# Gate and up products of four feed-forwards as seven block products, inner channels in four chunks

## What is computed

```python
D_FF_2 = 2816
def rmsnorm(x, g):
    xf = x.astype(jnp.float32)
    y = xf * lax.rsqrt(jnp.mean(xf * xf, axis=-1, keepdims=True) + EPS_2)
    return (y * g.astype(jnp.float32)).astype(x.dtype)
def swiglu_2(x, w_gate, w_up, w_down):
    return (jax.nn.silu(x @ w_gate) * (x @ w_up)) @ w_down
...
        h = h + 0.5 * swiglu_2(rmsnorm(h, ffn1_norm[i]), ffn1_w_gate[i], ffn1_w_up[i], ffn1_w_down[i])
...
        h = h + 0.5 * swiglu_2(rmsnorm(h, ffn2_norm[i]), ffn2_w_gate[i], ffn2_w_up[i], ffn2_w_down[i])
```

## Time and profile before

| | |
|---|---|
| median of three runs | 3580.78 us |
| the profiled execution's own time | 3585.51 us |
| its span, first to last instruction | 3583.7 us |
| instructions in the trace | 41702 |
| granted TensorE clock, mean | 0.992 of full |
| read from HBM | 288.22 MB, 81 GB/s over the span |

### The profile page before, as it was taken

One profiled execution on the slowest core, in us unless ns is written; L12 is line 12 of the kernel. 1 busy time (PEld: TensorE's weight loads), 2 busy tenths in 40 slices (PEclk: granted clock), 3 DMA queues, 4 the chain that ended last, 5 costly groups with the idle time before them and its releaser, 6 DMA issues. The chain is left out here.

```text
span 3583.7 us, 41702 instructions
## 1 busy us (share of the span) xinstructions
PE 3504.6 (98%) x15716; PEld 2778.8 (78%) x15740; DVE 1573.3 (44%) x2139; ACT 1285.5 (36%) x1802; POOL 443.9 (12%) x366
## 2 busy tenths in 40 slices
PE   9999999999999999999999999999999999999998
PEld 7787788877778886888876688887888886688886
DVE  3386433356643334333366733325333256733335
ACT  4243422234532224332343533225332333533324
POOL 0000111000211100221000022102221000022102
PEclk9999999999999999999999999999999999999999
DMA  4201233222022331333220233313333220133322
GB/s 146 88 1 30 82 94 103 103 71 77 30 82 94 101 104 59 96 97 110 81 72 18 65 96 97 116 57 97 97 96 107 82 84 18 53 95 99 111 71 77
DMA packets 78029, 292.06 MB, mean 81 GB/s; under 512 B 8656, under 2 KB 11472, under 8 KB 77648
## 3 DMA queue, kind: packets, MB, share of 16 engines
q1 hardware_dynamic: 77328, 289.31, 25.3%
q10 hardware_dynamic: 576, 1.05, 0.1%
HBM read 288.22 MB, written 2.10 MB: 81 GB/s over the span
## 5 line engine op out<-in xcount | busy, mean ns | idle before, releaser
L157 DVE TENSOR_TENSOR w_low<-w_raw,w_high 128x1024 fp32r<-128x1024 f32 (+4 forms) x513 | 672.5, 1311 | 1524.3 <-ACT w_high L152 1524.2
L191 PE MATMUL bank<-x_high,w_high 128*128 128x512 f32 x2856 | 1119.1, 392 | 18.8 <-DVE w_low L157 9.2
L193 PE MATMUL bank<-x_high,w_low 128*128 128x512 f32 x2856 | 1112.2, 389 | 0.0
L192 PE MATMUL bank<-x_low,w_high 128*128 128x512 f32 x2856 | 1111.9, 389 | 0.0
L152 ACT CAST w_high<-w_raw 128x1024 fp32r<-128x1024 f32 (+4 forms) x513 | 555.0, 1082 | 846.9 <-PE bank L193 838.9
L191 PEld LDWEIGHTS bank<-x_high,w_high 128*128 128x128 f32 x2856 | 536.5, 188 | 144.1 <-DVE w_low L157 14.0
L193 PEld LDWEIGHTS bank<-x_high,w_low 128*128 128x128 f32 x2856 | 536.3, 188 | 111.9
L192 PEld LDWEIGHTS bank<-x_low,w_high 128*128 128x128 f32 x2856 | 536.5, 188 | 111.3 <-issue 1.7
L191 PE MATMUL bank<-hidden_high,w_high 128*128 128x512 f32 x1056 | 410.8, 389 | 0.0
L192 PE MATMUL bank<-hidden_low,w_high 128*128 128x512 f32 x1056 | 410.8, 389 | 0.0
L193 PE MATMUL bank<-hidden_high,w_low 128*128 128x512 f32 x1056 | 410.8, 389 | 0.0
(11 more groups left out here) (543 smaller groups left out, 3473.5 us busy)
## 6 DMA issues: line engine op xcount, KB each, us to landing
w_raw<-in_stream SPq DMA_DIRECT2D x381, 512.0 KB, 3.5
w_raw<-in_stream SPq DMA_DIRECT2D x96, 704.0 KB, 4.0
w_raw<-in_stream SPq DMA_DIRECT2D x16, 384.0 KB, 3.1
w_raw<-in_stream SPq DMA_DIRECT2D x4, 576.0 KB, 3.7
dft_positions<-in_dft SPq DMA_DIRECT2D x2, 1024.0 KB, 4.7
w_raw<-in_stream SPq DMA_DIRECT2D x16, 128.0 KB, 2.0
out<-result SPq DMA_DIRECT2D x4, 512.0 KB, 2.7
h<-in_x ACTq DMA_DIRECT2D x4, 256.0 KB, 6.3
```

Of the source, the lines that this page charges most:

```text
L157: self.nc.vector.tensor_tensor(self.lo[:, j % 2, 0:size], self.raw[:, j % RAW_SLOTS, 0:size], self.hi[:, j % 2, 0:size].bitcast(F32), ALU. ...
L191: nc.tensor.matmul(out, lhs[0], rhs[0], start=start, stop=False)
L192: nc.tensor.matmul(out, lhs[0], rhs[1], start=False, stop=False)
L193: return nc.tensor.matmul(out, lhs[1], rhs[0], start=False, stop=stop)
```

## The change

In the four stages the first two pairs of tiles (`CLASSIC`) stay as they were. The other twenty are computed as a product of 2 by 2 blocks with seven block products and not eight: block rows are the gate tile and the up tile, inner blocks the two halves of the input channels, block columns the two halves of the tokens. A pair's four weight blocks of 128 x 512 are `a11`, `a12` (gate) and `a21`, `a22` (up). VectorE makes four sums of them (`sum_one` to `sum_four`, three of them in the raw slots), seven of these eight blocks (a unit each) are split by ScalarE and VectorE into rings of six, and a block product is 4 x 3 matmuls of 256 columns. The four matching sums of the input are made once per stage from a fresh normalised copy of `h` (`x_made`). Partial results are taken from PSUM by ScalarE (`copy_out`, four of 256 columns) and put together by VectorE (`gate_left`, `up_right`, `gate_right`). The hidden tile's product is two operations of 256 columns.

The 22 pairs are cut into chunks of 6, 6, 5 and 5; behind each chunk come its 8 down jobs (768 or 640 columns), each 18 or 15 matmuls into `bank[6]` or `bank[7]`, and each is added to `h`. The stage is written out without hardware loops. The weight stream is packed in the new order. Before each chunk behind the first, the splits and sums of the next chunk's first pair are made beside the last down jobs. What each GpSimd instruction does stays: two of 512 columns per pair.

```diff
+CHUNKS = (6, 6, 5, 5)
+CLASSIC = 2
+UNITS = 6
...
-def rms_ffn_stage(nc, C, scale, gain=None, summed=None, after=None, p_dram=None):
+def rms_ffn_stage(nc, C, scale, norm, gain=None, summed=None, after=None, p_dram=None):
...
+        hid = sb("hidden_parts", [P, max(CHUNKS), 2, T], F32R)
+        hhi, hlo = hid[:, :, 0, :], hid[:, :, 1, :]
+        thi, tlo = (sb(n, [P, 4, HALF_T, HALF], F32R) for n in ("x_sums_high", "x_sums_low"))
+        uhi, ulo = (sb(n, [P, UNITS, HALF_T * P], F32R) for n in ("units_high", "units_low"))
+        s_one = sb("w_sum", [P, HALF_T * P])
+        part = sb("products", [P, 4, HALF])
+        p1, u2, p5, u3 = (part[:, i, :] for i in range(4))
...
+        t_raw = [x_upper[:, :, left], x_upper[:, :, right], x_lower[:, :, right], x_lower[:, :, left]]
+        T1, T3, T2, T4 = range(4)
...
+        def unit_raw(f, kind):
+            a11, a12, a21, a22 = blocks(f)
+            return (a11, a12, a11, s_one[:, :], a21, a12, a22)[kind]
...
+                def product(f, kind, bank, high, low, start):
+                    u = unit_at(f, kind)
+                    pe.wait_ge(S.unit_low, 7 * strassen(f) + kind + 1)
+                    for q in range(HALF_T):
+                        whi, wlo = (w[:, u, q * P:(q + 1) * P] for w in (uhi, ulo))
+                        first, last = start and q == 0, q == HALF_T - 1
+                        nc.tensor.matmul(bank, whi, high[:, q, :], start=first, stop=False, skip_group_check=True)
+                        nc.tensor.matmul(bank, whi, low[:, q, :], start=False, stop=False, skip_group_check=True)
+                        mm = nc.tensor.matmul(bank, wlo, high[:, q, :], start=False, stop=last, skip_group_check=True)
+                    mm.then_inc(S.used, 1)
+                def pair(f):
+                    g = strassen(f)
+                    a, b, e = (C.bank[3 * (f % 2) + i][:, left] for i in range(3))
+                    upper, lower = slice(0, HALF_T), slice(HALF_T, DT)
+                    pe.wait_ge(S.hid_ready, f - 1)
+                    product(f, 0, a, C.xhi[:, upper, left], C.xlo[:, upper, left], True)
+                    if g == 0:
+                        pe.wait_ge(S.gate_in, 2)
+                    product(f, 1, e, C.xhi[:, lower, left], C.xlo[:, lower, left], True)
+                    pe.wait_ge(S.copied, 4 * g + 1)
+                    if g == 0:
+                        pe.wait_ge(S.t_low, T2 + 1)
+                    product(f, 2, a, thi[:, T2, :, :], tlo[:, T2, :, :], False)
+                    product(f, 3, b, thi[:, T1, :, :], tlo[:, T1, :, :], True)
+                    pe.wait_ge(S.copied, 4 * g + 2)
+                    product(f, 4, a, thi[:, T3, :, :], tlo[:, T3, :, :], False)
+                    pe.wait_ge(S.copied, 4 * g + 3)
+                    product(f, 5, b, C.xhi[:, lower, right], C.xlo[:, lower, right], False)
+                    pe.wait_ge(S.copied, 4 * g + 4)
+                    if g == 0:
+                        pe.wait_ge(S.t_low, T4 + 1)
+                    product(f, 6, a, thi[:, T4, :, :], tlo[:, T4, :, :], False)
...
+                for f in range(CLASSIC):
+                    classic(f, 0)
+                    classic(f, 1)
+                for c, n in enumerate(CHUNKS):
+                    for f in range(max(CLASSIC, first_pair(c)), first_pair(c + 1)):
+                        pair(f)
+                    down(c, 0, range(0, n - 1))
+                    down(c, 1, range(0, 3))
+                    down(c, 0, range(n - 1, n))
+                    down(c, 1, range(3, n))
+                    for d in range(2, DT):
+                        down(c, d, range(n))
                 keep_warm(nc, C, C.bank[0], 10)
...
+                def unit(f, kind):
+                    g = strassen(f)
+                    u = 7 * g + kind
+                    if kind in (0, 1):
+                        arrived(act, up_job(f, 0))
+                    elif kind == 6:
+                        arrived(act, up_job(f, 1))
+                    else:
+                        act.wait_ge(S.summed, 4 * g + (3, 1, 2, 4)[kind - 2])
+                    if u >= UNITS:
+                        act.wait_ge(S.used, u - UNITS + 1)
+                    nc.scalar.copy(uhi[:, u % UNITS, :], unit_raw(f, kind)).then_inc(S.unit_high, 1)
...
+                for t in range(DT):
+                    at = x_upper if t < HALF_T else x_lower
+                    nc.scalar.activation(at[:, t % HALF_T, :], C.h[:, t, :], ACT.Identity,
+                                         scale=norm(t)).then_inc(S.x_made, 1)
+                high(2, 2)
+                rstd_chain(nc, C, act, S, C.bank[summed or 6])
+                silu(0)
+                sums_high(T1)
+                sums_high(T3)
+                high(3, 3)
+                sums_high(T2)
+                sums_high(T4)
+                hidden_high(0)
+                f = CLASSIC
+                unit(f, 0)
+                unit(f, 1)
+                silu(1)
+                for kind in range(2, UNITS):
+                    unit(f, kind)
+                hidden_high(1)
+                for c, n in enumerate(CHUNKS):
+                    for f in range(max(CLASSIC, first_pair(c)), first_pair(c + 1)):
+                        last = f == first_pair(c + 1) - 1
+                        i, j = 2 * CLASSIC + DT * c, down_job(c, 0)
+                        bank = [C.bank[3 * (f % 2) + i] for i in range(3)]
+                        if f > CLASSIC:
+                            act.wait_ge(S.added, 3 * strassen(f))
+                        copy_out(f, 1, bank[0], p1)
+                        if f > first_pair(c) and f > CLASSIC:
+                            silu(f - 1)
+                        unit(f, 6)
+                        if last:
+                            high(i, j)
+                        else:
+                            act.wait_ge(S.used, 7 * strassen(f) + 2)
+                            unit(f + 1, 0)
+                        copy_out(f, 3, bank[0], u2)
+                        if not last:
+                            unit(f + 1, 1)
+                        copy_out(f, 4, bank[1], p5)
+                        if last:
+                            high(i + 1, j + 1)
+                        else:
+                            unit(f + 1, 2)
+                        if f > CLASSIC:
+                            act.wait_ge(S.hid_ready, f)
+                        copy_out(f, 5, bank[0], u3)
+                        if not last:
+                            unit(f + 1, 3)
+                        if f > first_pair(c) and f > CLASSIC:
+                            hidden_high(f - 1)
+                        if not last:
+                            unit(f + 1, 4)
+                            unit(f + 1, 5)
+                    silu(f)
+                    hidden_high(f)
+                    for d in range(DT):
+                        if d + 2 < DT:
+                            high(2 * CLASSIC + DT * c + d + 2, down_job(c, d + 2))
+                        elif c == len(CHUNKS) - 1 and d == DT - 2 and base + jobs < len(W.sizes):
+                            high(2 * CLASSIC + DT * (c + 1), jobs)
+                        if c < len(CHUNKS) - 1 and d == DT - 3:
+                            for kind in range(UNITS):
+                                unit(first_pair(c + 1), kind)
+                        if c == len(CHUNKS) - 1:
+                            act.wait_ge(S.residual_done, DT * c + d + 1)
+                            after.high(nc, C, act, S, d)
+                            after.square(nc, C, act, S, d, gated)
...
+                for f in range(FT):
+                    pool.wait_ge(S.gate_ready, f + 1)
+                    nc.gpsimd.tensor_tensor(gated[:, f % 2, :], gated[:, f % 2, :], C.rstd[:, :],
                                             ALU.mult).then_inc(S.gate_scaled, 1)
-                    pool.wait_ge(S.hid_high, u + 1 + 4 * k)
-                    at = bass.ds(u + 4 * k, 1)
-                    nc.gpsimd.tensor_tensor(hlo[:, at, :], hidden[:, u % 2:u % 2 + 1, :],
-                                            hhi[:, at, :].bitcast(F32), ALU.subtract).then_inc(S.hid_low, 1)
-                repeat(pool, FT, finish)
...
...
+                def sum_one(f):
+                    nc.vector.tensor_tensor(s_one[:, :], a21, a22, ALU.add).then_inc(S.summed, 1)
+                def sum_three(f):
+                    nc.vector.tensor_tensor(a21, a11, a21, ALU.subtract).then_inc(S.summed, 1)
+                def sum_two(f):
+                    nc.vector.tensor_tensor(a11, s_one[:, :], a11, ALU.subtract).then_inc(S.summed, 1)
+                def sum_four(f):
+                    nc.vector.tensor_tensor(a12, a12, a11, ALU.subtract).then_inc(S.summed, 1)
...
+                dve.wait_ge(S.x_made, HALF_T)
+                nc.vector.tensor_tensor(t_raw[T1], t_raw[T3], t_raw[T1], ALU.subtract).then_inc(S.t_made, 1)
+                dve.wait_ge(S.x_made, DT)
```

(83 more changed lines are left out.)

250 lines of the change are left out of this document (164 added, 86 removed).

## The result

The changed kernel takes **3650.45 us** (median of 4 runs, 3645.82 to 3655.06) against 3580.48 for the kernel before in the same sessions: ratio **1.0197**, 95% interval 1.0181 to 1.0212. The profiled execution took 3650.3 us, 64.8 more than that of the kernel before (3585.5). Lines from about 189 on stand four to some 330 lines further down in the new file: `three` is now L195 to L197, the block products are L1018 to L1020.

What follows compares the result with a forecast made beforehand. TensorE, 98% busy, was taken to bound the kernel before. Terms -64.8 + 48 (waits within chunks) + 4 + 32 + 7 + 6 = +32 us on 3585.5; forecast 3613 us, the profiled run lying 4.7 above the median; range 3550 to 3660.

Steps and rivals of the forecast that it cites:

- TensorE's term: Block pairs: 84 matmuls of 256 columns take 10.07 us instead of 10.88, saving 64.8 us over four stages.
- Rivals 3 and 4: Block products: weight loads not hidden, about 3970 us (chance 0.01); matmuls slowed to 129.5 ns, 3630 us (0.02).
- VectorE's loop: Middle pairs: VectorE, held by two GpSimd turns, takes 11.5 us; TensorE waits 1.42 us before product 6.
- Rival 1: Middle pairs: GpSimd's turns fall into VectorE's waits, loop at or under 10.07 us, 3552 us; chance 0.24.
- Rival 2: Middle pairs: waits add 0.05 us to each of 17 operations, loop 12.3 us, 3645 us; chance 0.15.
- What a turn is worth: Block pairs: each GpSimd operation costs VectorE 1.12 us; 0.62 of the scaling's lands on the chain.
- Stage start: Start of each stage: late low parts for job 3 and product 2 of the first pair 4.8 us late, +32 us.
- clock: After the 4.8 us wait at a stage's start: lower TensorE clock costs 1.7 us per stage, +7 us.
- Chunk end: End of the five-tile chunks: last hidden tile 0.5 us late in two chunks of each stage, +4 us.
- last chunk: Last chunk's down jobs: chain of 3.5 to 3.9 us against 3.4, hand-over 1.5 us late, +6 us.
- Loads hidden: Weight loads by DMA: same bytes, slots freed a pair ahead, so they stay hidden and cost nothing.
- the signs named: Timeline: loop 11.5 us, low parts' mean over 0.75, some 1.8, wait before product 6, matmuls 120 ns apart, product 2 late.

Runs made afterwards that it cites:

- e1: Changed kernel without GpSimd's second multiplication by `rstd` in the twenty block pairs: 3614.36 us, ratio 1.0101 to the kernel before.
- e2: Changed kernel, block pairs: GpSimd's multiplication by `rstd` kept, the hidden tile's low part set to zero by a GpSimd memset: 3586.81 us, ratio 1.0022.
- e5: Changed kernel plus one GpSimd multiplication per block pair that reads `rstd` from SBUF and writes an unread scratch tile: 3691.09 us, ratio 1.0306.
- e6: Changed kernel plus two GpSimd memsets per block pair, which only write a scratch tile: 3650.68 us, ratio 1.0197.
- e7: Changed kernel with VectorE adding a finished down-job bank to `h` before making the next low part: 3624.27 us, ratio 1.0116.
- b2: Changed kernel with Silu after unit 6, first copy before `hidden_high(1)`, residual before low part, and `rstd` applied to the down result on VectorE: 3553.67 us, ratio 0.9924.

## Why the prediction was right and where it was wrong

The direction, the time within the range and the mechanism of the pairs held; the loss was put at 32 us in the profiled execution and is 64.8. By its own steps:

- **TensorE's term, -64.8**: right. Where nothing waits six pairs take 60.47 us, 10.08 each against 10.07 forecast, half banks, strided inputs and weight loads included. Rivals 3 and 4 are out.
- **VectorE's loop, 11.5 us**: right in kind and place, 0.2 short. The bank, product and releaser are the ones named, and so is unit 6's low part as the operation held by the scaling; the other held one is `up_right`. The wait is 1.22 us shown and 1.48 in start-to-start time where 1.42 was forecast, plus 0.15 at one more product. The missing 0.2 is one wait inside VectorE: `sum_four` writes what unit 1's low part, the operation right ahead of it, has read, and starts 0.78 behind it (1548.38 to 1549.16) where the sum has 0.60. Chunks 2 to 4 lose 5.33 + 2 x 3.73 = 12.8 us a stage against 10.08 a pair, forecast 4.4 + 2 x 3.0: +9.5 us in all, the smaller part of the miss. e1, e2, e5 and e6 bear out that it is GpSimd's turns. Rival 1 (turns fall into waits) is out: 1.6 us of them are in the 11.70. Rival 2 (12.3 from 0.05 at each operation) is out as well: most of VectorE's operations that meet no turn start 0.60 behind each other, as forecast.
- **What a turn is worth**: 1.12 us of VectorE each, of which the scaling's was to put 0.62 on the chain. Measured 0.70 (11.70 to 11.00), near it; the low part's at least 0.92 (11.00 to 10.08, where TensorE takes over).
- **Stage start, +32, and clock, +7**: right in sum. Up to the end of chunk 1, 16 of the 80 pairs, the forecast was 32 + 7 + 4 x (0.3 + 1.4) - 64.8 / 5 = +32.8; measured +31.3 (two plain and four block pairs take 75.7, 72.3, 76.4 and 73.6 us, where six pairs took 67.1, 65.4, 68.9 and 65.4). The two named waits are there. Product 2 is 3.04 late in the first stage and 4.4 in the other three, forecast 4.8. Job 3 is late by 2.49, 1.45, 1.35 and 1.45, forecast 3.0 with `gain` and 2.1 without. The clock took more than forecast and makes up for them: behind each of product 2's waits the matmuls of 256 columns stand 0.21 apart instead of 0.12, for 3.7 and 3.5 us in the first two stages and 5.1 and 6.1 in the others (granted clock 0.79 over 8 us, then 0.64 and 0.58, which is the lower level of 1.2 GHz within time at 2.4), 1.6, 1.6, 2.3 and 2.8 us lost where 1.7 was forecast. Job 3's wait has such a stretch in the first stage (2.49 us idle, 0.43 apart in place of 0.23, 1.6 us lost) and in no other (1.35 to 1.45 us idle, granted clock 1.00).
- **Chunk end, +4, and last chunk, +6: the step that failed.** The down jobs and the hand-over came at +40.7 (31.0 + 9.7) against 10. What the two terms named came as forecast: the last hidden tile is 0.4 late in each chunk of five (0.52 and 0.34 between starts in place of 0.23, 3.3 us in all; gone in e1), and the next stage starts 6.4 us later in all. What failed is a term put at nothing, the wait for a **bank** in the down jobs: 32 waits, 26.1 us from start to start. The prediction looked for a late hidden tile and for a late hand-over; it did not follow VectorE's order against the banks. Before the change a tile had two down jobs, 15 us, so the low part that VectorE makes ahead of a residual cost nobody anything. Now a tile is one job of 4.08 or 3.40 us, the two banks alternate, and the residual behind a low part comes 0.63 (six tiles) to 1.05 us (five; once 1.33) too late at the third job of a chunk. In the last chunk each round takes 0.58 longer than its matmuls (3.98 - 3.40): that chain I had added up, 3.5 to 3.9 us against 3.4, and then charged only its end instead of every job. e7 shows it: the residual moved ahead of the low part gives back 26.2 of the 40.7. The other 3.3 us are the clock again, counted once per stage start and nowhere else: after the hand-over of stages 1 and 3 (2.69 us idle in the first) the next stage's first job takes 7.19 and 7.14 us instead of 5.5, at a granted clock of 0.79 over 8 us where the kernel before had 1.00.
- **Loads hidden**: right; none of TensorE's waits shown above hangs on a transfer, and in the whole list of waits two do, 2.4 us of ScalarE's.
- Of the signs named, the loop (11.70), the low parts' mean (0.779), the place and releaser of the wait, the matmuls' 120 ns and the chunk of six as long as six pairs before (65.8 against 65.3) are there; held low parts last 1.4 us and not 1.8.

The expected 64.8 us are really gained on TensorE, and given back twice over: 51 us in chunks 2 to 4, 44 in the starts and first chunks (31.3 + 13.0), 41 in down jobs and hand-over, less 7 that changed outside of these stages in this execution. That the loss is as large as this saving is chance.

What stays open: b2's down jobs take 3.6 us more per stage than before the change (123.5), and its first six pairs 4.2 (stages 2 and 4) and 7.5 us (with `gain`) more than TensorE's own 62.1. Four banks for the down jobs were not tried.

## What to carry to other kernels

When TensorE gets less work per tile, everything that was hidden per tile is charged again: for each bank, add up what its emptying engine has in front of that emptying, and compare it with one tile's new time, in every phase and not only in the one that was rewritten. Before a GpSimd operation is left beside a busy VectorE, ask what it reads: here each 512 column operation that reads SBUF cost 0.7 to 1.1 us of VectorE. Three moved lines and a per-token factor moved to the result made the change a gain of 0.8% instead of a loss of 2.0%: 44 us by the orders, 52 by the factor. And do not mend the wait that is shown before knowing whose loop sets the pace.
